# The first layers of three feed-forwards computed with seven half products in place of eight

## The reference, cut to what matters

```python
def sqrelu_mlp(hn, w1, w2):            # first block, w1 1024 x 4096, 512 tokens
    u = hn @ w1.astype(hn.dtype)
    u = jnp.square(jax.nn.relu(u))
    return u @ w2.astype(hn.dtype)
...
        h = h + swiglu(rmsnorm_2(h, norm_ffn[i]), ffn_w_in[i], ffn_w_out[i])   # i = 0, 1; inner width 2816
```

## Time and profile before

| what | value |
|---|---|
| median of three runs | 2085.11 us (2080.94 to 2085.74) |
| the profiled execution, its own time | 2085.97 us |
| its span, first to last instruction | 2083.9 us |
| mean granted TensorE clock | 0.978 of 2.4 GHz |
| TensorE matmuls | 11498 |

### The profile page before, as it was taken

The page is one execution under the profiler, slowest core; times in us unless marked ns, Lnnn a source line. Parts: engine busy times, 40 slices in busy tenths (PEclk is TensorE's granted clock), DMA queues, the critical chain, the costliest instruction groups (busy, mean ns, idle before and its releaser), DMA issues.

```text
span 2083.9 us, 28508 instructions
## 1 busy us (share of the span) xinstructions
PE 2007.6 (96%) x11498; PEld 1719.7 (83%) x11498; DVE 1055.4 (51%) x1353; ACT 745.3 (36%) x941; POOL 249.3 (12%) x208
## 2 busy tenths in 40 slices
PE   8999989999999999999999999999997899999996
PEld 6788766788888878999999999998884588888885
DVE  6668765544444544133443434346887444434435
ACT  4449734423132443223332222224444432222222
POOL 2012230200000210013200000001254010000001
PEclk9999999999999998998999999999998899999998
DMA  4223111222222221111222222223121022222221
GB/s 174 101 81 113 62 60 61 81 101 81 101 101 81 101 82 54 68 41 41 81 82 101 82 101 81 102 81 121 61 92 32 21 101 82 100 101 82 100 101 61
DMA packets 27823, 174.67 MB, mean 84 GB/s; under 512 B 4409, under 2 KB 4537, under 8 KB 7762
## 3 DMA queue, kind: packets, MB, share of 16 engines
q1 hardware_dynamic: 25680, 167.32, 22.6%
q0 software_dynamic: 1888, 5.90, 0.9%
q10 hardware_dynamic: 162, 0.10, 0.0%
HBM read 171.19 MB, written 4.78 MB: 84 GB/s over the span
## 4 chain that ended last, share of the span: by engine, by line
issue 58%; PE 30%; POOL 4%; DVE 3%; ACT 3%; DMA 1%; SPq 0%; POOLq 0%; DVEq 0%; ACTq 0%
PE lin L451 18%; POOL squares L634 3%; PE aux L2278 1%; PE aux L1307 1%; DMA w_raw<-in_weights 1%; PE lin L1509 1%; PE lin L1262 1%; ACT w_hi L363 1%; PE lin L2248 1%; PE aux L2262 1%; POOL w_lo L370 1%; PE aux L1291 1%; POOL r_t L1952 1%; PE aux L2126 1%; PE aux L2274 0%
## 5 line engine op out<-in xcount | busy, mean ns | idle before, releaser
L451 PE MATMUL lin<-v_hi,w_hi 128*128 128x264 f32 (+1 forms) x1664 | 555.6, 334 | 2.6 <-DVE gq_t L1772 1.4
L451 PE MATMUL lin<-v_hi,w_lo 128*128 128x264 f32 (+1 forms) x1664 | 553.3, 333 | 0.0
L451 PE MATMUL lin<-v_lo,w_hi 128*128 128x264 f32 (+1 forms) x1664 | 552.0, 332 | 0.0
L370 DVE TENSOR_TENSOR w_lo<-w_raw,w_hi 128x2048 fp32r<-128x2048 f32 (+1 forms) x144 | 328.5, 2281 | 184.5 <-ACT w_hi L363 184.2
L451 PE MATMUL lin<-x_hi,w_hi 128*128 128x512 f32 (+1 forms) x1160 | 408.4, 352 | 13.4 <-DVE tmp L546 6.5
L451 PE MATMUL lin<-x_hi,w_lo 128*128 128x512 f32 (+1 forms) x1160 | 406.7, 351 | 0.0
L451 PE MATMUL lin<-x_lo,w_hi 128*128 128x512 f32 (+1 forms) x1160 | 406.3, 350 | 0.0
L363 ACT ACTIVATE w_hi<-w_raw 128x2048 fp32r<-128x2048 f32 (+1 forms) x155 | 293.0, 1890 | 279.8 <-PE lin L451 269.1
L451 PEld LDWEIGHTS lin<-v_hi,w_hi 128*128 128x128 f32 x1664 | 315.2, 189 | 35.8 <-issue 3.1
L451 PEld LDWEIGHTS lin<-v_lo,w_hi 128*128 128x128 f32 x1664 | 315.1, 189 | 32.0 <-issue 0.5
L451 PEld LDWEIGHTS lin<-v_hi,w_lo 128*128 128x128 f32 x1664 | 314.9, 189 | 30.7
(11 more groups left out here) (391 smaller groups left out, 2408.1 us busy)
## 6 DMA issues: line engine op xcount, KB each, us to landing
w_raw<-in_weights SPq DMA_DIRECT2D x155, 1024.0 KB, 4.8
rel_by_distance<-rel_by_distance POOLq DMA_DIRECT2D x1, 2599.5 KB, 20.9
rel_bias<-rel_by_distance POOLq DMA_DIRECT2D x8, 264.0 KB, 3.0
h<-in_x_t SPq DMA_DIRECT2D x4, 512.0 KB, 8.2
out_t<-h SPq DMA_DIRECT2D x4, 512.0 KB, 2.8
o_t<-in_mem_t POOLq DMA_DIRECT2D x1, 1024.0 KB, 5.1
cst<-in_consts SPq DMA_DIRECT2D x1, 512.0 KB, 9.8
col<-in_cols ACTq DMA_DIRECT2D x1, 67.0 KB, 5.8
```

The costliest lines, as they stand in the source:

```text
L370: does.tensor_tensor(w_lo[:, s, 0:n], w_raw[:, s, 0:n], w_hi[:, s, 0:n].bitcast(F32), ALU.subtract).then_inc(sem("w_lo_ready"), 1)
L451: last = nc.tensor.matmul(o, a, b, start=(k % (L.kc // k_banks) == 0 and p == 0), stop=((k + 1) % (L.kc // k_banks) == 0 and p == 2))
```

## The change

Each unit of the first layers is cut in blocks: two halves of k (4 tiles of 128 rows) by two column tiles; the weights of a unit are stored as A11, A12, A22, A21 (`quad_unit`; 512 columns of the buffer each). The tokens are cut in two halves, first and second. A block of results is then the product of a 2x2 by a 2x2 block matrix. Strassen's scheme in Winograd's form needs seven products of half size, where the plain way needs eight. It needs sums of operands ahead of the products and sums of products behind them:

- Sums of weights, for every unit (`quad_sum`, GpSimd): S3, then A21+A22 in place, S2, S4, each of 128 x 512; and GpSimd makes the lo part of two of the four blocks (128 x 1024). ScalarE makes hi in four pieces (`quad_hi`: 512, 1024, 512 and 1536 columns), VectorE lo in three (`quad_lo`: 512, 512 and, last, 1536 columns of the sums, which gives `w_lo_ready`).
- Sums of the normed input, once for a feed-forward (`act_quad_operand`, `dve_quad_operand`).
- Products (`pe_quads`): seven of 12 matmuls each, over 256 or 264 columns, into seven PSUM banks, in the order p1 p6 p2 p7 p5 p4 p3 (in a feed-forward's first unit p1 p5 p2 p6, the sum of squares, p4 p7 p3).
- Sums behind: ScalarE copies p1; VectorE adds in four instructions (`dve_quad_top`, `_mid`, `_low`, `_last`), of which the last and the relu or silu work are done one unit later. `relu` and the square are one VectorE instruction.
- The loops over the units of these layers, and over layers in front of them, are written out.

The core of the diff:

```diff
+        def quad_sum(pool, unit, step):
+            q = quad_seq[unit]
+            if step == 4:
+                pool.wait_ge(sem("quad_w_hi"), 3 * q + 2)
+                nc.gpsimd.tensor_tensor(w_block(w_lo, unit, 1, 3), w_block(w_raw, unit, 1, 3),
+                                        w_block(w_hi, unit, 1, 3).bitcast(F32), ALU.subtract)\
+                    .then_inc(sem("quad_w_lo_pool"), 1)
+                return
+            a11, a12, a22, a21 = (w_block(w_raw, unit, x, x + 1) for x in range(4))
+            s3, s2, s4 = (w_sum[:, x * BLOCK_W:(x + 1) * BLOCK_W] for x in range(3))
+            if step == 0:
+                pool.wait_ge(sem(f"w_loaded{unit % 2}"), 16 * (unit // 2 + 1))
+                if q:
+                    pool.wait_ge(sem("w_lo_ready"), quad_units[q - 1] + 1)
+            else:
+                pool.wait_ge(sem("quad_sum"), 4 * q + step)
+            out_t, x, y, op = ((s3, a21, a11, ALU.subtract), (a21, a21, a22, ALU.add),
+                               (s2, a21, a11, ALU.subtract), (s4, a12, s2, ALU.subtract))[step]
+            nc.gpsimd.tensor_tensor(out_t, x, y, op).then_inc(sem("quad_sum"), 1)
...
+        def quad_hi(act, unit, part, tiles_before=0):
...
+            if part == 0:
+                act.wait_ge(sem("lin_done"), tiles_before)
+                act.wait_ge(sem(f"w_loaded{unit % 2}"), 16 * (unit // 2 + 1))
+                nc.scalar.activation(w_block(w_hi, unit, 0, 1), w_block(w_raw, unit, 0, 1), ACT.Copy)\
+                    .then_inc(sem("quad_w_hi"), 1)
+            elif part == 1:
+                nc.scalar.activation(w_block(w_hi, unit, 1, 3), w_block(w_raw, unit, 1, 3), ACT.Copy)\
+                    .then_inc(sem("quad_w_hi"), 1)
+            elif part == 2:
+                act.wait_ge(sem("quad_sum"), 4 * q + 2)
+                nc.scalar.activation(w_block(w_hi, unit, 3, 4), w_block(w_raw, unit, 3, 4), ACT.Copy)\
+                    .then_inc(sem("quad_w_hi"), 1)
+            else:
+                act.wait_ge(sem("quad_sum"), 4 * q + 4)
+                nc.scalar.activation(ws_hi[:, unit % 2, :], w_sum[:, :], ACT.Copy).then_inc(sem("w_hi_ready"), 1)
...
+        def quad_lo(dve, unit, part):
...
+            elif part == 2:
+                dve.wait_ge(sem("quad_w_hi"), 3 * q + 3)
+                nc.vector.tensor_tensor(w_block(w_lo, unit, 3, 4), w_block(w_raw, unit, 3, 4),
+                                        w_block(w_hi, unit, 3, 4).bitcast(F32), ALU.subtract)\
+                    .then_inc(sem("quad_w_lo"), 1)
+            elif part == 3:
+                dve.wait_ge(sem("quad_w_lo_pool"), q + 1)
+                dve.wait_ge(sem("w_hi_ready"), unit + 1)
+                nc.vector.tensor_tensor(ws_lo[:, unit % 2, :], w_sum[:, :], ws_hi[:, unit % 2, :].bitcast(F32),
+                                        ALU.subtract).then_inc(sem("w_lo_ready"), 1)
...
+        def act_quad_operand(act, N, t, par):
...
+            if t >= 4:
+                nc.scalar.activation(v_raw[:, t, 0:n], N.tile(t), ACT.Copy, scale=N.gain(t))\
+                    .then_inc(sem("quad_gained"), 1)
+            a = v_hi[:, t, 0:n if t >= 4 else hf], N.tile(t) if t >= 4 else h_half(N, t, 0)
+            nc.scalar.activation(*a, ACT.Copy, scale=N.gain(t)).then_inc(sem("operand_hi"), 1)
+            act_squares(act, N, t, par)
+            act.wait_ge(sem("quad_raw"), KD * N.quads0 + t + 1)
+            if t < 4:
+                nc.scalar.activation(v_hi[:, t, hf:n], v_raw[:, t, hf:n], ACT.Copy, scale=N.gain(t))\
+                    .then_inc(sem("quad_hi"), 1)
...
+                nc.scalar.activation(vt_hi[:, :, t - 4, 0:hf], vt_raw[:, :, t - 4, 0:hf], ACT.Copy)\
+                    .then_inc(sem("quad_hi"), 1)
...
+        def dve_quad_operand(dve, N, t):
...
+                nc.vector.scalar_tensor_tensor(v_lo[:, t, hf:n], v_raw[:, t, hf:n], N.gain(t),
+                                               v_hi[:, t, hf:n].bitcast(F32), ALU.mult, ALU.subtract)\
+                    .then_inc(sem("quad_lo"), 1)
+                return
+            j = t - 4
+            t3, t2, t4 = (vt_raw[:, x, j, 0:hf] for x in range(3))
+            dve.wait_ge(sem("quad_gained"), 4 * N.quads0 + j + 1)
+            link(dve, nc.vector.scalar_tensor_tensor(t3, h_half(N, j, 1), N.gain(j), v_raw[:, t, hf:n],
+                                                     ALU.mult, ALU.subtract))
+            link(dve, nc.vector.scalar_tensor_tensor(t2, h_half(N, j, 0), N.gain(j), t3, ALU.mult, ALU.subtract))
+            nc.vector.tensor_tensor(t4, v_raw[:, t, 0:hf], t2, ALU.subtract).then_inc(sem("quad_raw"), 1)
+            dve.wait_ge(sem("quad_raw"), done)
+            dve.wait_ge(sem("operand_hi"), N.tiles0 + t + 1)
+            nc.vector.tensor_tensor(v_lo[:, t, 0:n], v_raw[:, t, 0:n], v_hi[:, t, 0:n].bitcast(F32), ALU.subtract)\
+                .then_inc(sem("operand_lo"), 1)
+            dve.wait_ge(sem("quad_hi"), done)
+            nc.vector.tensor_tensor(vt_lo[:, :, j, 0:hf], vt_raw[:, :, j, 0:hf], vt_hi[:, :, j, 0:hf].bitcast(F32),
+                                    ALU.subtract).then_inc(sem("quad_lo"), 1)
...
+        def pe_quads(pe, L, N=None):
...
+                bank, b = QUAD_BANK[name]
+                if name == "p1":
+                    pe.wait_ge(sem("quad_w_lo"), 2 * q + 1)
+                elif name == "p5":
+                    pe.wait_ge(sem("quad_w_lo"), 2 * q + 2)
+                elif name in ("p2", "p4"):
...
+                elif name in ("p1", "p6", "p2"):
+                    pe.wait_ge(sem("quad_top"), q)
+                elif name in ("p7", "p5", "p4"):
+                    pe.wait_ge(sem("quad_low"), q)
+                else:
+                    slot, before, _ = L.tile(t % 2, 0, t // 2)
+                    pe.wait_ge(sem(f"lin_taken{slot}"), before)
+                for k in range(4):
+                    if name in ("p1", "p5"):
+                        x = [v[:, k, 0:hf] if name == "p1" else v[:, k, hf:n] for v in (v_hi, v_lo)]
+                    elif name in ("p2", "p3"):
+                        x = [v[:, 4 + k, 0:hf] if name == "p2" else v[:, 4 + k, hf:n] for v in (v_hi, v_lo)]
+                    else:
...
+                                              start=(k == 0 and p == 0), stop=(k == 3 and p == 2))
+                if name == "p3":
+                    mm.then_inc(sem("lin_done"), 2)
+                else:
...
+            for t in range(L.units):
+                if L.unit0 + t in first_quads:
+                    for name in QUAD_FIRST:
+                        if name == "p4":
+                            pe.wait_ge(sem("lin_taken1"), L.tile0 // 2)
+                            pe_squares(pe, N)
+                        elif name == "p7":
+                            pe.wait_ge(sem("square_root"), N.roots0 + 1)
+                        product(t, name)
+                else:
+                    for name in QUAD_STEADY:
+                        product(t, name)
...
+        def dve_quad_top(dve, L, t):
+            hf = L.n // 2
+            dve.wait_ge(sem("quad_done"), quad_done(L.unit0 + t, "p6", "p2"))
+            dve.wait_ge(sem("quad_s1"), quad_seq[L.unit0 + t] + 1)
+            nc.vector.tensor_tensor(tmp[:, 0:2, 0:hf], spread_row(tmp[:, 0, hf:2 * hf]), aux[:, 1:3, 0:hf],
+                                    ALU.add)\
+                .then_inc(sem("quad_top"), 1)
...
+        def dve_quad_mid(dve, L, t):
...
+            nc.vector.tensor_tensor(tmp[:, 0:2, hf:n], spread_row(tmp[:, 0, 0:hf]), lins[:, 1:3, 0:hf], ALU.add)\
+                .then_inc(sem("quad_mid"), 1)
...
+        def dve_quad_low(dve, L, t):
...
+            nc.vector.tensor_tensor(tmp[:, 2, 0:n].rearrange("p (x n) -> p x n", x=2), spread_row(tmp[:, 1, hf:n]),
+                                    lins[:, 0:2, 0:hf], ALU.add).then_inc(sem("quad_low"), 1)
...
+        def dve_quad_last(dve, L, t):
...
+            dve.wait_ge(sem("lin_done"), tile + 2)
+            dve.wait_ge(sem("quad_low"), quad_seq[L.unit0 + t] + 1)
+            nc.vector.tensor_tensor(tmp[:, 1, hf:n], tmp[:, 0, hf:n], lins[:, 3, 0:hf], ALU.add)\
+                .then_inc(sem(f"lin_taken{slot}"), 1)
+            dve.wait_ge(sem(f"lin_taken{slot}"), before + 1)
...
+            def squared(t):
+                dve_quad_last(dve, L, t)
+                for m in range(2):
+                    r = tmp[:, 1 + m, 0:S1]
+                    nc.vector.scalar_tensor_tensor(tmp[:, 3 - m, 0:S1], r, 0.0, r, ALU.max, ALU.mult)\
+                        .then_inc(sem("u_made"), 1)
...
+            def low(t):
+                for m in range(2):
+                    k = 2 * t + m
+                    dve.wait_ge(sem("u_hi"), base + k + 1)
+                    nc.vector.tensor_tensor(one(u_lo, k, 0, S1), tmp[:, 3 - m, 0:S1], one(u_hi, k, 0, S1).bitcast(F32),
+                                            ALU.subtract).then_inc(sem("u_lo"), 1)
...
+                    squared(t - 1)
```

(42 more changed lines are left out.)

298 lines of the change are left out of this document (223 added, 75 removed).

## The result

The changed kernel takes 2196.14 us (median; 2193.59 to 2199.37), the kernel before 2084.74 us in the same comparison: a ratio of 1.054, 95% interval 1.052 to 1.056. It is 111 us slower. The forecast was 2155 us, 69 to 70 us slower, with a range from 2060 to 2215: the sign and the mechanism hold, the size is 41 us short. The time lies inside the range, but 1 us above the stretch from 2120 to 2195 that had the chance of 0.64.

A forecast was written before the change was run, and what follows sets the result against it. Before the change TensorE's columns bound the feed-forwards; after it, the ring of waits between GpSimd and VectorE would. 2085.97 + 51 for the parts + 18 for the input's sums = 2155 us, range 2060 to 2215.

The forecast's parts named there:

- TensorE's saving: First-layer units: 84 short matmuls save 1.18 us a unit, 1.45 in up0; 76.7 us if nothing else becomes the bound.
- the turns: VectorE's two-SBUF-input instructions and GpSimd's shut each other out, whole instructions at a time: GpSimd holds 1.16 us, VectorE 0.57.
- a ring: First-layer units, from one 1536-column quad_lo to the next: 13.8 us in ff1, 13.2 in up, 13.3 at 528 columns.
- two cases: VectorE gets four or three two-SBUF instructions done under GpSimd's five: 13.1 or 13.5 us in up, 13.8 or 14.2 in ff1.
- the signs named: Expected in the profile: VectorE's squares, gate and low averaging 1.2 us or more, GpSimd's sums 1.5 to 1.8, top and mid 0.7.
- Packed turns: Rival for the units: engines alternate without gaps, 11.3 us a unit in ff1, 10.8 in up; total 2057 us; chance 0.11.
- the input's sums: Layers ahead of the feed-forwards: xo +12 us, all together +18, with 8 to 30 as ends.
- The written-out forecast of a part: A part of L units: 9.8 us to unit 1's quad_lo, L - 2 rings, then six products, 8.5 us; together +51 us.
- its likeliest case: The main forecast for the whole kernel, rings of 12.7 to 14.3 us: 2120 to 2195 us, chance 0.64.
- No holding up: Rival for the units: VectorE and GpSimd overlap freely and TensorE stays the bound; 2042 us; chance 0.09.
- without loss: Rival for the units: turns packed with no gap, 11.3 us in ff1, 10.8 in up; total 2057 us; chance 0.11.
- Worse: Rival: lower TensorE clock gives 2275 us; a ring of 14.5 and 30 us for the input's sums give 2215; chance 0.06.

The follow-up runs named there:

- the run with all three edits: Changed kernel with sums in three slots, ScalarE's 1024-column hi early, and the 1024-column lo on VectorE: 2091.6 us, 1.004 of the kernel before.
- plain preparation: Changed kernel with the feed-forwards' input prepared as before the change, without sums of its halves and quarters: 2166.5 us, 1.040 of the kernel before.
- plain preparation and GpSimd writing only: Changed kernel with the input prepared as before the change and GpSimd's five instructions a unit as memsets: 2032.2 us, 0.975 of the kernel before.
- GpSimd writing only: Changed kernel with GpSimd's four sums and its lo in each unit replaced by memsets, waits unchanged: 2052.3 us, 0.986 of the kernel before.

## Why the prediction held, and where it fell short

**TensorE's saving: right.** There are 12,602 matmuls, and with the turns taken away a ring is 9.95 and 10.20 us, where 84 x 0.1187 and 84 x 0.1211 gave 9.97 and 10.17.

**The turns: right, shown from both sides.** The ring, 13.3 us forecast for up0, is 13.31; 13.2 for up1, 13.23; 13.8 for ff1, 13.55. That it fits to 0.01 us in up is luck. The forecast lay between two cases, four of VectorE's two-SBUF instructions done under GpSimd's five (13.1 us) and three (13.5), with most weight on four. In up it is three: the fourth, L413, first waits 1.23 us for ScalarE's copy, which the prediction had put out of the way, and is issued just behind GpSimd's lo. In ff1 it is four. Inside the ring two more sizes were off and partly cancel: GpSimd's step with its own wait is 1.38 us undisturbed and not 1.46, so its five instructions end 8.8 us after they start in up and 9.2 in ff1, not at 9.1 and 9.4; and VectorE's undisturbed instructions follow at 0.73 to 0.80 us, not 0.69. Of the signs named, squares have a mean of 1.00 us and the gate one of 0.79, and low in up stays at 0.69, none of them at 1.2 or more: the gate begins under GpSimd's first sum and low after its lo, so the turns fall on other instructions. Packed turns needed another order of the lists: of the rival's 11.3 and 10.8 us the run with all three edits reached 10.0 to 10.7 and 11.0 to 11.1, with VectorE in place of GpSimd for the lo.

The Trainium skill (SBUF — State Buffer, Who interferes with whom) says that a VectorE instruction with two SBUF inputs contends with a GpSimd instruction that reads SBUF and not with one that only writes it. The runs agree on both: 2.83 us beside the reading lo, 0.69 beside the memsets.

**What was mis-sized.** VectorE's reciprocals mark the stages: one behind xo, one behind ff1, one behind g_out, one behind up0, one behind a_out, one at the end. In the kernel before, the second to the last:

```profile
750.95 3.45 DVE L703 RECIPROCAL scale_d<-scale_d 128x528 f32<-128x528 f32 x1 [0.99 <-ACT scale_tok L687]
...
1047.43 3.45 DVE L703 RECIPROCAL scale_d<-scale_d 128x528 f32<-128x528 f32 x1 [1.23 <-ACT scale_d L684]
...
1435.65 3.45 DVE L703 RECIPROCAL scale_d<-scale_d 128x528 f32<-128x528 f32 x1 [0.54 <-ACT scale_tok L687]
...
1703.82 3.35 DVE L703 RECIPROCAL scale_d<-scale_d 128x512 f32<-128x512 f32 x1 [1.00 <-ACT scale_d L684]
...
2071.86 3.35 DVE L703 RECIPROCAL scale_d<-scale_d 128x512 f32<-128x512 f32 x1 [4.95 <-ACT scale_d L684]
```

and in the changed kernel all six:

```profile
407.93 3.34 DVE L892 RECIPROCAL scale_d<-scale_d 128x512 f32<-128x512 f32 x1
...
787.95 3.45 DVE L892 RECIPROCAL scale_d<-scale_d 128x528 f32<-128x528 f32 x1 [0.99 <-ACT scale_tok L876]
...
1095.31 3.44 DVE L892 RECIPROCAL scale_d<-scale_d 128x528 f32<-128x528 f32 x1
...
1504.30 3.45 DVE L892 RECIPROCAL scale_d<-scale_d 128x528 f32<-128x528 f32 x1 [0.54 <-ACT scale_tok L876]
...
1784.66 3.34 DVE L892 RECIPROCAL scale_d<-scale_d 128x512 f32<-128x512 f32 x1
...
2181.11 3.35 DVE L892 RECIPROCAL scale_d<-scale_d 128x512 f32<-128x512 f32 x1 [4.01 <-ACT scale_d L873]
```

With 387.66 of the earlier trace rows, the changed kernel's marks come later and later:

- Up to and including the layer in front of a feed-forward (what ends in the first, third and fifth mark; the mixers in it are unchanged): + 20.3, + 10.9 and + 12.2 us, 43.3 together. Forecast was 18, for the input's sums.
- From those marks to the second, fourth and sixth: + 16.7, + 20.8 and + 28.4, 65.9 together. Forecast was 51.

*The layers in front, 25 us short.* With plain preparation the same marks stand at 397.29, 777.54, 1077.30, 1488.20, 1755.50 and 2154.34, so these layers still cost 12 (+ 9.6, + 3.3, - 0.9), and the input's sums are 31 by the trace (28 to 30 by the times), not 18. One tile of xo shows why:

```profile
381.22 0.67 DVE L640 TENSOR_TENSOR h<-h,lin 128x512 f32<-128x512 f32 x1
...
384.24 1.66 DVE L761 TENSOR_TENSOR v_lo<-v_raw,v_hi 128x512 fp32r<-128x512 f32 x1
385.82 3.15 DVE L764 TENSOR_TENSOR vt_lo<-vt_raw,vt_hi 128x768 fp32r<-128x768 f32 x1
...
389.49 0.68 DVE L640 TENSOR_TENSOR h<-h,lin 128x512 f32<-128x512 f32 x1
...
385.31 2.84 POOL L364 TENSOR_TENSOR w_lo<-w_raw,w_hi 128x1024 fp32r<-128x1024 f32 x1
```

I gave such a tile 5.1 us, from VectorE's own durations and its waits for ScalarE. It takes 8.27: v_lo is held by the squares (1.66), vt_lo by GpSimd's lo (3.15 for an instruction that takes 0.94 when free), and the first unit's quad_lo stands in the list as well. I had found the turns and applied them to the units only; the same pair of engines meets in the input's stage too, where GpSimd squares each tile and makes the first unit's sums. Other tiles are 3.44 us in place of 2.8, and 5.5 to 7.1. With GpSimd's unit instructions writing only, the input's sums still cost 20 to 23 us by the times and 24 by the marks (34.6 against 10.4 us in these layers). But GpSimd's squares still read there and hold VectorE up as before:

```profile
383.54 1.69 DVE L761 TENSOR_TENSOR v_lo<-v_raw,v_hi 128x512 fp32r<-128x512 f32 x1
...
383.29 1.39 POOL L799 TENSOR_TENSOR squares<-squares,tmp 128x512 f32<-128x512 f32 x1 [4.11 <-ACT tmp L780]
```

The chain of small instructions itself was not costed too low. In xo of that run the first four tiles come every 3.45 us with a v_lo held for 0.8 us (1.29 in place of 0.49), and a last one takes 5.48 with one held for 1.0; less these holds that is an estimated 2.65 and 4.5 us, where the forecast had 2.8 and 5.1. So the step that fell short is the one that left the hold-ups out of the input's stage.

The other 12 us remain with plain preparation. They fall where VectorE splits the first unit's weights in three quad_lo in place of one, which went at nothing into the sum; with plain preparation and GpSimd writing only, 10 are left (+ 4.6, + 3.6, + 2.2 by that run's marks), so in xo half of the 9.6 goes with GpSimd's reads. No run took these three instructions out alone, so that they are the cause isn't shown.

*The feed-forwards, 15 us short.* Two thirds of it is a hand-over that I had not seen. TensorE's first matmul of a second layer, and the instruction of VectorE ahead of it:

```profile
1338.56 0.36 PE L558 MATMUL lin<-x_hi,w_hi 128*128 128x264 f32 x1 [1.49 <-issue]
...
1338.03 0.43 DVE L1985 TENSOR_TENSOR tmp<-tmp,lin 128x264 f32<-128x264 f32 x1
```

The second layer's first tile is written to the banks that VectorE's `last` (L1985) releases, and `last` can only follow the unit's last product. TensorE idles 0.56 to 1.60 us at each of the ten passages, 9.8 us in all; with GpSimd writing only 0.56 to 0.57 us each, 5.6 in all, are left, and they belong to the order of the sums alone. So the 24 us left in the run with plain preparation and GpSimd writing only are 10 in the layers in front, 5.6 here and some 8 for the reciprocals and the rest. The written-out forecast of a part ended with "six products of the last unit" and nothing behind them. It went at nothing into the sum: the prediction asked whether the second layer's operands are ready, and not whether its banks are free. The rest, about 5 us, lies in the seven later parts, each 0.1 to 2.3 us more over the kernel before than forecast, the hand-over not counted; the first parts, counted from the marks, are together 1 us shorter than forecast. The largest piece is ff1d, 48.1 us where ff1b and ff1c take 46.1 and 46.4 and 45.9 was forecast. There the granted clock is 0.57 from 716 to 724 us, after an idle stretch of 1.97 us and with one of 0.83 us in it, and the matmuls of the last unit follow at 0.213 us in place of 0.119 until it is back.

**The clock.** The mean granted clock is 0.960, 0.978 before. From 386 to 408 us, in and around the 9.4 us stretch without matmuls, it was 0.77; inside the parts it is 0.96 to 0.98. The forecast costed this at nothing in its likeliest case. With GpSimd writing only it is 0.973. Apart from some 2 us in ff1d, what the clock cost in microseconds was not measured.

**The rivals.** "No holding up" falls by the durations of 1.5 to 2.8 us, "without loss" by rings of 13.2 to 13.6 us where they need 10.8 and 11.3. "Worse" holds for the input (31 us by the marks, 30 as it said) but not in its ring of 14.5. Nearly all that was missed lies outside the rings: in the layers in front, put at 18 us, and at the hand-overs, put at nothing.

## What to carry to other kernels

Before moving work to GpSimd, list every VectorE instruction with two SBUF inputs that can run beside it, in every stage and not only in the loop, and count whole instructions as turns; a GpSimd instruction with VectorE's critical one waiting behind it costs the most, and can be cheaper on VectorE even when that is the fuller engine. For an exchange of matmuls for sums, write down the hand-over at both ends of each layer: the last sum of the last unit now stands where the last matmul stood. And a buffer that one engine frees only after its last instruction makes a ring; but taking the ring away gives back only what the lists behind it let through (0.6 of 3.1 us here, 2.2 with the lists reordered and the lo moved).

## What the runs showed of the hardware

- A GpSimd memset beside VectorE's two-SBUF instructions costs neither anything (0.69 us); 1248 columns take 1.19 us (4.76 / 4), less than the 1.30 us of a two-input sum of 512 columns.
- A VectorE instruction issued a moment after GpSimd's ends 0.54 to 0.57 us after it for 512 and 528 columns, whatever GpSimd's length: in the ring at 1259.72 us 2.83 us beside a lo of 2.40, and 1.78 and 1.79 beside sums of 1.64 and 1.62.
- With GpSimd writing only, 264-column fp32r matmuls follow at 0.121 us through 76 us of uninterrupted work (628 in the window of up0b below), and so do their weight loads, as in the earlier trace rows; the rings of 9.95 us are 84 of 256 columns at 0.118. The finer products cost TensorE nothing of their own.

```profile
1184.00:1260.00 76.00, 76.00 (x628) 76.00 (x627) 53.52 (x72) 37.38 (x51) 43.23 (x41) 1.00 0.31 110
```
